# Attention of a four-layer diffusion backbone: the maxima one block of queries ahead instead of one head ahead, placed between the score blocks

## The reference

```python
for i in range(DEPTH):
    hc, hl = mod_norm(xc, ...), mod_norm(xl, ...)          # context rows, latent rows
    # project to q, k, v and a gate; rms norms and rotary by layer
    s = einsum('bqhd,bkhd->bhqk', q, k) * scale            # MLA adds the rotary part
    p = softmax(s)                                         # SWA: band mask, sink in the sum
    o = einsum('bhqk,bkhd->bqhd', p, v)
    x = x + gt * ((o * silu(gate)) @ w_out[i])
```

## Time and profile before

| | us |
|---|---|
| median of 3 runs (lowest, highest) | 3885.57 (3880.24, 3885.69) |
| the profiled execution's own time | 3885.78 |
| its span, first to last instruction | 3884.0 |
| busy: PE, PE weight loads | 3544.3 (91%), 2040.4 (53%) |
| busy: DVE, ACT, POOL | 2490.0 (64%), 2190.3 (56%), 1091.3 (28%) |
| mean granted TensorE clock, share of 2.4 GHz | 0.984 |

### The profile page before, as it was taken

One profiled execution on the slowest core, in us unless ns is written; L12 is line 12 of the kernel. 1 busy time (PEld: TensorE's weight loads), 2 busy tenths in 40 slices (PEclk: granted clock), 3 DMA queues, 4 the chain that ended last, 5 costly groups with the idle time before them and its releaser, 6 DMA issues. The chain is left out here.

```text
span 3884.0 us, 71972 instructions
## 1 busy us (share of the span) xinstructions
PE 3544.3 (91%) x27916; PEld 2040.4 (53%) x27916; DVE 2490.0 (64%) x3536; ACT 2190.3 (56%) x2859; POOL 1091.3 (28%) x931
## 2 busy tenths in 40 slices
PE   6999899999999988999899988888999998898888
PEld 3554455555455555555555555555555445555544
DVE  6436677777357468888655428886642667777744
ACT  5424677777444358888733227776333457676761
POOL 0000344444220025555521002223200014444442
PEclk9999999999999999999999999999999999999999
DMA  6227433232112342332012434332112652222111
GB/s 250 64 86 228 105 76 82 57 83 63 63 34 76 113 125 62 74 71 67 23 68 72 124 101 101 97 96 58 52 51 90 187 145 42 57 47 57 41 52 60
DMA packets 375890, 330.05 MB, mean 85 GB/s; under 512 B 247168, under 2 KB 294976, under 8 KB 374112
## 3 DMA queue, kind: packets, MB, share of 16 engines
q1 hardware_dynamic: 375648, 326.66, 31.1%
HBM read 235.37 MB, written 91.23 MB: 84 GB/s over the span
## 5 line engine op out<-in xcount | busy, mean ns | idle before, releaser
L798 PE MATMUL bank<-H_hilo,w_hilo 128*128 128x512 f16 (+1 forms) x5760 | 1044.7, 344 | 11.0 <-DVE w_hilo L1048 7.8
L2309 ACT ACTIVATE p_f<-bank 128x1024 f32<-128x1024 f32 (+2 forms) x768 | 744.1, 969 | 485.2 <-PE bank L2247 421.1
L2247 PE MATMUL bank<-q_slots,k_slots 96*128 96x512 f16 (+7 forms) x3968 | 949.2, 369 | 7.4 <-PEq L1199 4.4
L2062 DVE TENSOR_REDUCE max_parts<-bank 128x1 f32<-128x512 f32 (+1 forms) x1248 | 795.7, 663 | 247.7 <-PE bank L1993 240.3
L798 PEld LDWEIGHTS bank<-H_hilo,w_hilo 128*128 128x128 f16 x5760 | 563.4, 98 | 492.1 <-DVE w_hilo L1048 8.8
L2313 ACT ACTIVATE p_hi<-bank 128x1024 f16<-128x1024 f32 (+2 forms) x768 | 741.1, 965 | 0.0
L2427 POOL TENSOR_TENSOR p_lo<-p_f,p_hi 128x1024 f16<-128x1024 f32 x240 | 534.5, 2227 | 648.4 <-ACT p_hi L2313 648.4
L2374 DVE TENSOR_TENSOR p_lo<-p_f,p_hi 128x1024 f16<-128x1024 f32 (+1 forms) x528 | 599.8, 1137 | 156.7 <-ACT p_hi L2313 155.8
L1993 PE MATMUL bank<-k_slots,q_slots 96*128 96x512 f16 (+4 forms) x1392 | 487.5, 372 | 70.8 <-DVE max_parts L2062 53.4
L2247 PEld LDWEIGHTS bank<-q_slots,k_slots 96*128 96x128 f16 (+2 forms) x3968 | 369.1, 99 | 314.5 <-issue 29.1
L2216 PE MATMUL bank<-cq_hilo,p_hi 128*128 128x129 f16 x3200 | 338.8, 221 | 37.9 <-ACT o_lo_hi_den L2327 22.7
(11 more groups left out here) (207 smaller groups left out, 3721.6 us busy)
## 6 DMA issues: line engine op xcount, KB each, us to landing
ada_w<-in_w_ada SPq DMA_DIRECT2D x48, 768.0 KB, 6.2
gate<-z_ring SPq DMA_DIRECT2D x32, 640.0 KB, 3.3
gate_rows<-gate SPq DMA_DIRECT2D x32, 640.0 KB, 4.0
q_slots<-q_mla SPq DMA_DIRECT2D x64, 240.0 KB, 3.2
k_mla<-H_hilo SPq DMA_DIRECT2D x64, 224.0 KB, 3.2
k_slots<-k_mla SPq DMA_DIRECT2D x64, 224.0 KB, 4.4
cq_hilo<-v_scratch SPq DMA_DIRECT2D x64, 224.0 KB, 4.1
v_lo_hi_one<-v_scratch SPq DMA_DIRECT2D x64, 224.0 KB, 4.3
```

What stands on the lines that cost most here:

```text
L798: ins = pe.matmul(dst, lhs(a, k), rhs(b, k), start=(k == 0 and n == 0), stop=(k == nk - 1 and n == 2))
L2062: dve.tensor_reduce(mx[:, par, t, c:c + 1], entry_bank(b, k)[:, 0:n], AX.X, ALU.max).then_inc(s_red.h, 1)
L2247: ins = pe.matmul(dst, lhs, rhs, start=(m == 0), stop=(m == len(ops) - 1), skip_group_check=swa)
L2309: act.activation(p32[:, p % 2, 0:cols], src, ACT.Exp, scale=scale).then_inc(s_p32.h, 1)
```

## The change

The entries of a head are no longer all issued while the head before is worked through. Only unit 0's and a part of unit 1's are (`ahead`). The rest of unit 1's, unit 2's and their turns are issued in the first steps of the head itself (`own`). There are two or three entries in each step of MLA and GQA. The first entry of a step now stands between the two score blocks, the second behind the scores, and the others behind the value product; DVE takes two entries ahead of `p_lo` instead of one. ACT copies the output bank between `p_f` and `p_hi`. POOL's list of `p_lo` steps gets step 1 in MLA and GQA, and steps 0, 2, 4 and 6 in SWA. In SWA the double entries become two single ones. The rotary rows of the keys are loaded once for each slot.

```diff
-        for dst, src in ((Q[0:MLA_QK, b, 0], q[0:MLA_QK]), (Q[0:MLA_QK, b, 1], q[MLA_QK:2 * MLA_QK]),
-                         (K[0:HD, b, 0], k[0:HD]), (K[0:HD, b, 1], k[HD:2 * HD]),
-                         (K[HD:MLA_QK, b, 0], self.KP_m[0:ROPE]), (K[HD:MLA_QK, b, 1], self.KP_m[ROPE:2 * ROPE])):
+        moves = [(Q[0:MLA_QK, b, 0], q[0:MLA_QK]), (Q[0:MLA_QK, b, 1], q[MLA_QK:2 * MLA_QK]),
+                 (K[0:HD, b, 0], k[0:HD]), (K[0:HD, b, 1], k[HD:2 * HD])]
+        if rope_keys:
+            moves += [(K[HD:MLA_QK, b, 0], self.KP_m[0:ROPE]), (K[HD:MLA_QK, b, 1], self.KP_m[ROPE:2 * ROPE])]
...
+        a_, b_, c_ = maxima_of(0), maxima_of(1), maxima_of(2)
+        out_step = [{3: 1, 4: 2}, {8: 0}] if swa else [{5: 1, 6: 2}, {10: 0}]
...
         if swa:
-            base = c_ + a_[:3] + [("turn", 2)] + a_[3:] + b_[:3] + [("turn", 0)] + b_[3:]
+            own = [b_[4:6], b_[6:8] + c_[:1], c_[1:] + [turn(1)], [turn(2)], [], [], [], [], []]
+            ahead = [[], [], a_[:1], a_[1:2], a_[2:4], a_[4:7], a_[7:] + b_[:1], [turn(0)] + b_[1:3], mod + b_[3:4]]
         else:
-            base = c_ + a_[:lag] + [("turn", 2)] + a_[lag:] + b_[:lag] + [("turn", 0)] + b_[lag:]
+            own = [b_[5:7], b_[7:9] + c_[:1], c_[1:] + b_[9:11], b_[11:] + [turn(2)], [turn(1)]] + [[]] * 8
+            ahead = [[]] * 4 + [a_[:2], a_[2:4], a_[4:6], a_[6:8], a_[8:10], a_[10:] + b_[:1], mod + b_[1:2],
+                                [turn(0)] + b_[2:3], b_[3:5]]
...
-        early = [1, 1, 1, 1, 0, 0, 1, 2, 1] if swa else [1] * (NS - 1) + [0]
...
-        pooled = [] if swa else [3, 5, 7, 9, 11]
+        pooled = [0, 2, 4, 6] if swa else [1, 3, 5, 7, 9, 11]
...
 # PE, step p
                             for n, (kt, q0, nq, off, masks) in enumerate(blocks):
...
+                                if n == 0:
+                                    for k in todo[:1]:
+                                        emit_entry(pe, i, b, k)
+                            scored.then_inc(s_sc.h, 1)
+                            for k in todo[1:2]:
+                                emit_entry(pe, i, b, k)
-                            for k in todo[:early[p % NS]]:
-                                emit_entry(pe, npair, nb, k)
                         if (p >= 2 or not first) and (p < P2 or last):
                             pv(i, p - 2)
                         if p < P2:
-                            for k in todo[early[p % NS]:]:
-                                emit_entry(pe, npair, nb, k)
+                            for k in todo[2:]:
+                                emit_entry(pe, i, b, k)
...
 # ACT, step p: behind p_f
+                        if p >= 2 or not first:
+                            take_o(i, p)
+                        if p < P2:
...
                             act.activation(ph[:, slot[p], 0:cols], src, ACT.Exp, scale=scale).then_inc(s_ph.h, 1)
-                            if not (last and b == 1):
-                                for k in at_step[1 - b][p % NS]:
-                                    copy_rows(act, i + b, 1 - b, k)
+                            for k in items(b, p % NS, last):
+                                copy_rows(act, i, b, k)
...
 # DVE, step p
-                        for k in found[:early[p % NS]]:
-                            take_entry(dve, i + b, 1 - b, k)
+                        for k in found[:2]:
+                            take_entry(dve, i, b, k)
...
                         inverse(i, p, first)
-                        for k in found[early[p % NS]:]:
-                            take_entry(dve, i + b, 1 - b, k)
+                        for k in found[2:]:
+                            take_entry(dve, i, b, k)
```

More of the change, by code:

```diff
@@ L1750, in scores_of @@
                 if u == 2:
[L1751 to L1752 removed]
+                    found.append(("max", u, t, 0, PAST + LAT, CTX, []))
                 elif not swa:
@@ L1790, in attention @@
+        order = [e for step in ahead for e in step] + [e for step in own for e in step]
+        NE = len(order)
+        NM = NE - 3 - ada
+        stream, at_step = [[], []], [[], []]
         for b in range(2):
             for j in range(NS):
[L1792 to L1795, removed]
@@ L1796, in attention @@
-        count = lambda b, k, which: sum(e[0] in which for e in entries[b][:k])
-        nmax = [[count(b, k, ("max",)) for k in range(len(entries[b]) + 1)] for b in range(2)]
-        nturn = [[count(b, k, ("turn",)) for k in range(len(entries[b]) + 1)] for b in range(2)]
-        nbase = [[count(b, k, ("max", "turn", "ada")) for k in range(len(entries[b]) + 1)] for b in range(2)]
-        ring = [(b, k) for b in range(2) for k in range(len(entries[b]))]
-        if len(ring) % 2:
-            ring.append(None)
@@ L1803, in attention @@
-        place = {bk: n for n, bk in enumerate(ring) if bk}
-        turns = [e[1] for e in base if e[0] == "turn"]
-        turn_order = {u: n for n, u in enumerate(turns)}
-        turned_in = {j: nturn[0][k] for k, j in step_of[0].items() if swa and entries[0][k][0] == "turn"}
-        both = bank[2][:].rearrange("p b n -> p (b n)")
-        def entry_bank(b, k):
-            if not swa:
-                return MB[place[b, k] % 2]
-            if entries[b][k][0] != "turn":
-                return MB[0]
-            return SB[((1 - b) * NS + step_of[b][k]) % 2][:, 1]
+                made = [(0, e) for e in own[j]] + [(1, e) for e in ahead[j]]
@@ new lines, in attention @@
+                if j in out_step[b]:
+                    made.append((0, ("out", out_step[b][j])))
+                at_step[b].append(list(range(len(stream[b]), len(stream[b]) + len(made))))
+                stream[b] += made
+        count = lambda k, which: sum(e[0] in which for e in order[:k])
+        nmax = [count(k, ("max",)) for k in range(NE + 1)]
+        nturn = [count(k, ("turn",)) for k in range(NE + 1)]
+        turns = [e[1] for e in order if e[0] == "turn"]
+        turn_order = {u: n for n, u in enumerate(turns)}
@@ new lines, in attention, with head_of, items @@
+        ring = [(b, n) for b in range(2) for n in range(len(stream[b]))]
+        ring += [None] * (-len(ring) % R)
+        place = {bn: n for n, bn in enumerate(ring) if bn}
+        before_all = [e for step in ahead for e in step]
+        def head_of(i, b, n):
+            b += stream[b][n][0]
+            return i + b // 2, b % 2
+        def items(b, j, last):
+            if last and b == 1:
+                return [n for n in at_step[b][j] if stream[b][n][0] == 0 and stream[b][n][1][0] != "out"]
+            return at_step[b][j]
@@ L1815, in attention, with entry_bank @@
+        def entry_bank(i, b, n):
+            if isinstance(i, int) and i < 0:
+                return MB[sum(d for d, e in stream[b][:n]) % 2]
+            return MB[place[b, n] % R]
         P2 = 2 * NS
@@ new lines, in wait_bank @@
+        def wait_bank(pe, i, b, n):
+            if isinstance(i, int) and i < 0:
+                earlier = [m for m in range(n) if stream[b][m][0] == 1]
+                if len(earlier) >= 2:
+                    wait_taken(pe, i, b, earlier[-2])
+                return
+            m = place[b, n]
+            while True:
+                m -= R
+                if m < 0:
+                    m, i = m + len(ring), i - 1
+                if isinstance(i, int) and i < 0:
+                    pe.wait_ge(s_red.h, s_red.base + sum(e[0] == "max" for e in before_all))
+                    pe.wait_ge(s_mr.h, s_mr.base + sum(e[0] == "turn" for e in before_all))
+                    return
+                if ring[m] is not None and wait_taken(pe, i, *ring[m]):
+                    return
```

308 lines of the change are left out of this document (133 added, 175 removed).

## The result

The changed kernel takes 3970.12 us (median of 4 runs, 3967.81 to 3971.78), the one before 3882.90 (4 runs): ratio 1.0225, 95% interval 1.0207 to 1.0243. The forecast was 3918 in a range of 3790 to 3960. The sign was right. The loss was 85 to 87 us where 33 were forecast, and the time lies outside the range.

The account below looks back on a forecast made before the run. PE was taken to lead narrowly, so every added wait lands on the end. 15 heads +56, last head +8, stages ahead -27 and transfers -4 make +33 on 3885.6: 3918 us, range 3790 to 3960.

Parts of the forecast that it names:

- Wait 1: Turn 1 in the middle of step 4, MLA and GQA: PE waits 2.0 us a head for ACT's row copy.
- wait 2: Turn 0 in step 11, its bank wanted by b3 in step 12: PE waits 1.65 us in MLA, 1.8 in GQA.
- wait 3: Steps 1 to 3: POOL's `p_lo` holds DVE's negated maximum, reductions come late: 1.7 us a head in MLA, 2.6 in GQA.
- POOL in GQA: Layer 1: POOL's splits and other work make its `p_lo` of steps 7 and 8 late, 0.9 us a head.
- The spreading: Steps 5 to 11: PE runs without waiting on DVE; nearly all of 4.3, 6.1 and 4.8 us a head goes.
- PE's work: PE's own busy time a head, taken as 33.1 us in layer 0, 27.7 in layer 1, 32.1 in layer 3.
- the lock: `tensor_scalar` in a 2-port mode and GpSimd operations hold shared ports exclusively; without it the forecast is 20 to 30 us lower.
- the stages ahead: Ahead of attention, shorter tails: 8 us off layer 1 plus 3 for clock, 7 each layers 0 and 3, 2 layer 2.
- the transfers: Two rotary transfers a head less, first used in step 4 instead of 2, remove waits: -4 us.
- SWA at +1.0 us a head: Layer 2: about 5 us of waits in steps 0 to 4 and 1.3 elsewhere, against 4.9 before; ends -2.5 and +3.
- rival D: Slower by PE's clock: 2 us gaps followed by 1.2 GHz add 25 to 40 us to the forecast, 3950; chance 0.15.
- which step length hides: Output copy between `p_f` and `p_hi` delays `p_hi` by about 0.58 us in three steps a head, at no cost.

Follow-up runs that it names:

- e3: Changed kernel with the turns of layers 0, 1 and 3 moved away from their bank's next user, maxima ahead starting in step 5: 3857.06 us, ratio 0.9936.
- e4: Changed kernel with the negated maximum of layers 0, 1 and 3 made by a tensor_reduce instead of a tensor_scalar, nothing moved: 3920.05 us, ratio 1.0091.
- e6: Changed kernel with only the first 11 maxima entries between the projections ahead of layers 0 and 3, the rest in a tail: 3959.74 us, ratio 1.0201.
- e8: Kernel before the change, with the negated maximum of layers 0, 1 and 3 made by a tensor_reduce instead of a tensor_scalar: 3852.84 us, ratio 0.9927.
- e7: Changed kernel with ACT's copy of the output bank back behind `p_hi` and the row copies, in all layers: 3944.77 us, ratio 1.0163.
- e2: Changed kernel with POOL taking no `p_lo` in layer 2 (SWA), DVE taking them all: 3927.22 us, ratio 1.0123.

## Why the prediction was wrong

**The waits by head: right, with their places.** Wait 1 was put at 2.0 us (measured 1.66 and 2.01), wait 2 at 1.65 and 1.8 (1.47 and 1.50), wait 3 at 1.7 and 2.6 in two parts (1.3 and 2.0), POOL in GQA at 0.9 (0.6). e3 and e4 took them away one by one. The heads were forecast at 38.4, 35.0 and 37.4 us and took 38.4, 35.1 and 37.7. The spreading holds: in MLA steps 7 to 9 start 2.44 us apart. But two errors cancel in these sums, and that is luck. I took 33.1, 27.7 and 32.1 us for PE's work; the heads less all gaps over 0.06 us give 34.0, 28.9 and 33.2 after, 34.7, 29.0 and 34.1 before. So the waits that could vanish were 2.9, 3.4 and 4.3 us and not 4.3, 4.8 and 6.1, and the new ones were each a little shorter than forecast. Why PE needs 0.6, 0.2 and 0.8 us a head less between its gaps than before is not shown. Other than forecast, step 9 takes 2.65 us, since it has three entries, and steps 5 and 6 take 2.90 and 2.69 where they have out entries.

**Two sums that don't follow.** Without the lock, the prediction says, the forecast would be 20 to 30 us lower; its own second parts (1.1 us in 30 heads of MLA, 1.6 instead of 0.4 in 15 of GQA) make 51, and e4 gave 50. And for SWA 5 us of waits and 1.3 of the rest, against 4.9, make +1.4 a head, not +1.0: 6 us of the 21 missed in layer 2.

**Failed: the stages ahead, taken at -27 (and -4 for the transfers).** I read what PE waited for in the tail and took that for the stage's end. The stage ends when its last engine does. In MLA, where 7 us a layer were forecast, SP's stores of the keys were as late as the tail, and from the last projection to the first scores it took 8.1 to 8.7 us with a tail and without; e6 shows it from the other side. In layer 1, where 8 us and 3 for the clock were forecast, this stretch fell by 5.9, and in layer 2 it grew by 0.4: 6 us in place of 27. The first scores of layer 0 came 5.1 us sooner, but 4.5 of that is the projections' end, and with the stages of the kernel before e8's trace has them 4.0 sooner too. From the first scores to the first output copy 5 us came back over the four layers: the first head has the new waits as well (1.1 to 1.8 us a layer more), and in layers 0, 1 and 3 some 1 us more each was spent at 1.2 GHz, some half of which is lost. The 21 us of the tail and these 5 are the 26 of the 51 us missed. The transfers were mis-sized and misplaced: before, PE waited 11.7 us for the rotary rows (12 times, in the heads of layer 0), and after not at all.

**Failed: SWA at +1.0 us a head, where it was +2.4.** The prediction had DVE's `p_lo` and negated maximum run into POOL, and allowed 5 us of waits and 1.3 of the rest against 4.9 before. By the gaps there were 5.2, against 3.8 before: 1.4 of the 2.4 us. The other 1.0 is the clock. The prediction kept PE's fall to half clock as rival D for the layers with 2 us gaps and put none in layer 2, where gaps of 1.48 and 2.09 us came 4 us apart in nearly every head. PE's work there went from 20.1 to 21.1 us a head (clock 0.98 to 0.94), 15 of the 36 us.

**Failed: "which step length hides".** The output copy between `p_f` and `p_hi` cost some 25 us (e7), part of it inside layer 2's miss. It was priced by PE's slack in the step, but `p_hi` also starts POOL's `p_lo`, and where that ends DVE was waiting.

**The Trainium skill's rule** (SBUF — State Buffer, § Who interferes with whom) that wait 3 leaned on was borne out by e4: `tensor_scalar` was held up to 1.78 us, `tensor_reduce` with the same operands never over 0.16. The section also names the other pair seen here: a `tensor_tensor` with both inputs in SBUF against a GpSimd operation that reads SBUF. L2344 is one, 0.96 us on the mean with POOL beside it and 0.17 without (e2).

**Marks set in advance.** Met: steps 5 to 8 of MLA take 2.44 us each where they have two entries, PE ahead of L2003 waits mostly for L2084, L2069's longest is 1.78 us, layer 1's stage is over 545 us (566). Missed: L2069's mean is 0.67 us and not over 0.8; the waits for L2084 are 135 of 1.1 us and not 90 of 2; layer 3 took 605 us from its first scores, a little over 600.

## What to carry to other kernels

When an entry moves from behind the long operation to its middle, price it by the one who frees its buffer: a transposition that a third engine must copy away needs that engine's next free moment between it and the bank's next user. Before crediting a shorter tail, look at every engine that closes the stage, the DMA queue first. And where one engine's operation can hold another, whatever starts the first (here ACT's `p_hi`) can be on the critical path, and it pays to ask whether the held operation can be of another kind: that alone gave 50 us here and 29 in the kernel before (e4, e8).

## What the runs showed of the hardware

- A DVE `tensor_scalar` of 4 elements a partition took up to 1.78 us beside a POOL `tensor_tensor` and ended with it; the same by `tensor_reduce` took 0.154 to 0.158 us, 144 times of 144.
- The hold works both ways: in layer 1 POOL's L1982 on 256 columns took 1.53 us beside DVE's `p_lo` instead of 0.67, and L2407 1.60 instead of 0.62.
- Two gaps of PE of 1.48 and 2.09 us, 4.5 us apart, were followed by a stretch at 1.2 GHz in 10 of 13 cases in layer 2. Of 15 single gaps of 1.41 us in layer 0 (each some 5 us behind one of 0.7) only 4 were.
